# A two-block transformer kernel: matrix products on the stream before its norm, in the first stage of the latent attention and in the token pooling

## The reference

```python
def rmsnorm(x, g):
    y = x * lax.rsqrt(jnp.mean(x * x, axis=-1, keepdims=True) + 1e-6)
    return y * g

# end of the first block, start of the second
x = x + 0.5 * swiglu(rms_norm(x, ffn2_norm), ...)
x = rms_norm(x, final_norm)
h = concatenate([meta_tokens, x])                 # 16 + 512 tokens
a = rmsnorm(h, norm_mix_pre[0]);  lat = a @ w_dqkv # latents of the attention, 672 columns
...
# second layer of the second block
a = rmsnorm(h, norm_mix_pre[1])
# pool_mixer: 4 groups of 256 features, windows 2, 4, 8, 16
pooled[t, g] = sum(a[t-w+1 .. t, g]) / min(t + 1, w)
mixed = pooled - a
y = einsum('blgc,gcd->blgd', mixed, w_group) * scale
h = h + rmsnorm(y, norm_mix_post[1])
```

## Time and profile before

| | us |
|---|---|
| median of 3 runs (lowest, highest) | 2468.05 (2458.19, 2468.3) |
| the profiled execution's own time | 2468.25 |
| its span, first to last instruction | 2466.5 |
| PE busy, share of the span | 2308.9, 94% |
| DVE, ACT, POOL busy | 1069.0, 910.1, 998.1 |

### The profile page before, as it was taken

The page is one execution under the profiler, slowest core; times in us unless marked ns, Lnnn a source line. Parts: engine busy times, 40 slices in busy tenths (PEclk is TensorE's granted clock), DMA queues, the critical chain, the costliest instruction groups (busy, mean ns, idle before and its releaser), DMA issues.

```text
span 2466.5 us, 35997 instructions
## 1 busy us (share of the span) xinstructions
PE 2308.9 (94%) x14099; PEld 2027.3 (82%) x14099; DVE 1069.0 (43%) x1584; ACT 910.1 (37%) x1656; POOL 998.1 (40%) x758
## 2 busy tenths in 40 slices
PE   8999999999889899999988999799999938999999
PEld 6888887777677678888877888799999837999999
DVE  3313134564432242231356563562644475626354
ACT  4323235313353342222354453542433335424243
POOL 3445454532363344444531112244444432444443
PEclk9999999998899999999999999899999968999999
DMA  4333323321242123333211011133232201333221
GB/s 145 94 97 95 94 81 91 86 69 35 86 137 69 52 84 96 94 94 94 86 56 32 28 35 49 48 93 94 86 94 84 79 9 57 89 94 94 86 88 67
DMA packets 355686, 193.61 MB, mean 78 GB/s; under 512 B 7357, under 2 KB 350034, under 8 KB 355554
## 3 DMA queue, kind: packets, MB, share of 16 engines
q1 hardware_dynamic: 355026, 190.61, 26.4%
q10 hardware_dynamic: 528, 1.19, 0.2%
HBM read 189.67 MB, written 2.10 MB: 78 GB/s over the span
## 4 chain that ended last, share of the span: by engine, by line
PE 82%; DVE 11%; ACT 4%; issue 2%; DMA 0%; DVEq 0%; ACTq 0%; SPq 0%; POOL 0%
PE PS L544 22%; PE PS L546 22%; PE PS L548 22%; PE PS L1966 2%; PE PS L566 2%; PE PS L1984 1%; DVE u_conv L908 1%; PE PS L2038 1%; PE PS L2020 1%; ACT w_hi L490 1%; DVE g_conv L908 1%; PE PS L1155 1%; DVE hid L919 1%; PE PS L1567 1%; DVE u_conv L911 1%
## 5 line engine op out<-in xcount | busy, mean ns | idle before, releaser
L477 POOL TENSOR_TENSOR w_lo<-raw,w_hi 128x512 fp32r<-128x512 f32 (+4 forms) x743 | 976.4, 1336 | 1417.9 <-ACT w_hi L490 1417.9
L544 PE MATMUL PS<-XHI,w_hi 128*128 128x512 f32 (+2 forms) x2632 | 741.8, 332 | 41.0 <-DVE XLO L644 37.0
L490 ACT ACTIVATE w_hi<-raw 128x512 fp32r<-128x512 f32 (+4 forms) x743 | 412.5, 604 | 943.4 <-PE PS L548 879.4
L546 PE MATMUL PS<-XLO,w_hi 128*128 128x512 f32 (+2 forms) x2632 | 731.6, 328 | 0.0
L548 PE MATMUL PS<-XHI,w_lo 128*128 128x512 f32 (+2 forms) x2632 | 729.0, 327 | 0.0
L544 PEld LDWEIGHTS PS<-XHI,w_hi 128*128 128x128 f32 x2632 | 446.8, 190 | 97.4 <-issue 45.2
L546 PEld LDWEIGHTS PS<-XLO,w_hi 128*128 128x128 f32 x2632 | 444.7, 190 | 46.3 <-issue 2.9
L548 PEld LDWEIGHTS PS<-XHI,w_lo 128*128 128x128 f32 x2632 | 445.0, 190 | 43.6
L544 PE MATMUL PS<-h_hi,w_hi 128*128 128x512 f32 (+2 forms) x1056 | 282.3, 321 | 5.9 <-DVE h_lo L921 5.8
L546 PE MATMUL PS<-h_lo,w_hi 128*128 128x512 f32 (+2 forms) x1056 | 281.6, 321 | 0.0
L548 PE MATMUL PS<-h_hi,w_lo 128*128 128x512 f32 (+2 forms) x1056 | 281.5, 321 | 0.0
(11 more groups left out here) (294 smaller groups left out, 2404.3 us busy)
## 6 DMA issues: line engine op xcount, KB each, us to landing
raw<-in_ffn_w_up SPq DMA_DIRECT2D x132, 512.0 KB, 3.7
raw<-in_ffn_w_down SPq DMA_DIRECT2D x64, 512.0 KB, 3.8
raw<-in_ffn_w_gate SPq DMA_DIRECT2D x44, 512.0 KB, 3.8
raw<-in_w_in SPq DMA_DIRECT2D x25, 512.0 KB, 3.7
raw<-in_ffn_w_down SPq DMA_DIRECT2D x32, 384.0 KB, 3.4
raw<-in_xattn_w_kv SPq DMA_DIRECT2D x16, 512.0 KB, 3.7
raw<-in_w_out SPq DMA_DIRECT2D x8, 512.0 KB, 3.7
raw<-in_xattn_w_q SPq DMA_DIRECT2D x8, 512.0 KB, 4.4
```

Source lines behind the costliest of these rows:

```text
L477: ins = nc.gpsimd.tensor_tensor(d, r, h.bitcast(F32), ALU.subtract)
L490: ins = nc.scalar.activation(d, r, ACT.Copy)
L544: nc.tensor.matmul(ps, wh, ahi(k)[:, c:c + w], start=(k == 0), stop=False)
L546: nc.tensor.matmul(ps, wh, alo(k)[:, c:c + w], start=False, stop=False)
```

## The change

Two stages are rearranged; the arithmetic that is asked for stays the same.

In the first, PE's attention units are computed on the stream before `final_norm`, with the gains of `final_norm` and of the pre-norm multiplied into one (`fin_g`). Both norms' factors become one factor behind the product: the mean of squares of x times the `final_norm` gain, plus eps times the first norm's mean square. The meta tokens, which have no final norm, get their squares (`meta_sq`) and gained values (`meta_t`) early, in the first FFN. The splits of the stream's tiles move into the last units of the FFN, the second norm's squares are added up by DVE and summed by one `pe_norm` behind the second unit, and the final norm's own factor and the scaling of `X` by it are moved into the attention's steps (`dve_fin_x`).

In the second, PE multiplies the group weights with the stream before its norm and before the pooling, which commute with the product. The splits of `X` start in the post-norm. The factor and the window sums follow on the evacuated product (`grouped`), all on DVE; POOL's window sums and the tile `mixed` are gone.

```diff
-    PE_SUMMED = (S_FFN1, S_MLA, S_CF0, S_POOL, S_POOLP, S_CF1)
+    PE_SUMMED = (S_FFN1, S_CF0, S_POOL, S_POOLP, S_CF1)
...
+        (dve_rows, behind the copies of the gains)
+        link(nc.vector.tensor_tensor(meta_t[:, :, :], x_meta, x_meta, ALU.mult))
+        link(nc.vector.tensor_reduce(meta_sq[:, :], meta_t[:, :, :].rearrange("p k t -> p t k"), AX.X, ALU.add))
+        nc.vector.tensor_tensor(meta_t[:, :, :], x_meta, pre.to_broadcast([P, KD, META]), ALU.mult).then_inc(cols_ready, 1)
+        nc.vector.tensor_tensor(fin_g[:, :], column("final_norm", None, 0, KD), pre, ALU.mult).then_inc(cols_ready, 1)
...
+    def act_fin_split(act, m, j):
+        ...
+        nc.scalar.activation(XHI[:, m, META:S2], xt(m, 1), ACT.Identity, scale=fin_gain(m)).then_inc(x_hi, 1)
+        act_square(act, S_FIN, m, j, xt(m, 1), S1)
+    def dve_fin_split(dve, m, j):
+        ...
+        nc.vector.scalar_tensor_tensor(XLO[:, m, META:S2], xt(m, 1), fin_gain(m), XHI[:, m, META:S2].bitcast(F32), ALU.mult,
+                                       ALU.subtract).then_inc(x_lo, 1)
+        dve_acc(dve, S_FIN, m, j, S1)
     def act_fin(act):
-        act_sqrt(act, S_FIN, S1)
         for k in range(KD):
-            x_ready.wait(act, ("fin", k))
-            act_split(act, D_MLA, k, k, 2, G_PRE[0])
-            act_square(act, S_MLA, k, k, X[:, k, :], S2)
+            if k == KD // 2:
+                hi_to(act, PHASE["mla"] + 2)
+            act.wait_ge(acc_done, KD * S_MLA + k - 1)
+            nc.scalar.activation(sq[:, k % 2, 0:S1], xt(k, 1), ACT.Square, scale=G_FIN(k)).then_inc(sq_done, 1)
+        hi_to(act, PHASE["mla"] + 3)
+        act.wait_ge(norm_ms, S_MLA + 1)
+        act_rsqrt(act, sd[:, 0:S2], ms[:, 0:S2]).then_inc(norm_sd, 2)
     def dve_fin(dve, link):
-        dve_norm(dve, link, S_FIN, (PHASE["ffn2"] + 68) % 4, 1)
-        (per tile: scale X by gain and factor, L1716; dve_split)
+        (fin_ms from PSUM; ms of the stream = fin_ms * EPS, of the meta tokens EPS)
+        (per tile: acc += sq; then ms += mean of the second sum, and the Newton step)
+    FIN_X_AT = {14: 0, 24: 1, 34: 2, 44: 3, 54: 4, 64: 5, 70: 6, 74: 7}
+    def dve_fin_x(dve, link, x):
+        if x == 5:
+            dve.wait_ge(fin_sd, 1)
+            newton(link, fin_rn[:, :], fin_ms, rt[:, 0:S1], fin_rn[:, :])
+        if x in FIN_X_AT:
+            k = FIN_X_AT[x]
+            link(nc.vector.scalar_tensor_tensor(xt(k, 1), xt(k, 1), G_FIN(k), fin_rn[:, :], ALU.mult, ALU.mult))
...
     def pe_mla(pe):
-        pe_first_unit(pe, n, S_MLA, D_MLA, 2, n)
-        for j in range(1, 6):
+        for j in range(6):
+            if j == 0: pe.wait_ge(meta_lo, 1)
+            if j == 2: pe.wait_ge(norm_ms, S_FIN + 1)
             if j == 3:
                 pe.wait_ge(norm_ms, S_MLA + 1)
             pe_unit(pe, n + j, ...)
+            if j == 0: pe_norm(pe, S_FIN, (n + 2) % 4, 1).then_inc(norm_sum, 1)
+            if j == 1: pe_norm(pe, S_MLA, (n + 3) % 4, 2).then_inc(norm_sum, 1)
...
     def act_mla(act):
-        hi_to(act, n + 2)
-        act_sqrt(act, S_MLA, S2)
...
         act_m.inc(ins, "krope")
+        act_rsqrt(act, fin_rn[:, :], fin_ms).then_inc(fin_sd, 1)
         hi_to(act, n + 3)
...
     def pe_pool(pe):
-            if g == 1:
-                pe.wait_ge(norm_ms, S_POOL + 1)
-            (two pe_square of the group before)
+        pe.wait_ge(norm_ms, S_POOL + 1)
+        for m in range(KD):
             pe_square(pe, S_POOLP, SUMS, 2, m)
     def act_pool(act):
-        (per group: split mixed; evacuate to M and square the group before; hi_to(n + g + 1))
+        act_sqrt(act, S_POOL, S2)
+        for g in range(4):
+            hi_to(act, n + g + 2)
+            evacuate(g)                      # to grouped
+        for m in range(KD):
+            pool_mixed.wait(act, m)
+            act_square(act, S_POOLP, m, m, M[:, m, :], S2)
     def dve_pool(dve, link):
+        for k in range(3):
+            dve_split(dve, D_POOL, k, 2, G_PRE[1])
+        dve.wait_ge(acc_done, KD * (S_POOL + 1))
+        (ms)
+        for k in range(3, KD):
+            dve_split(dve, D_POOL, k, 2, G_PRE[1])
+        (Newton step)
+        for g, win in enumerate(WINDOWS):
+            for k in tiles:
+                pool_out(dve, k)
+                link(nc.vector.tensor_tensor(pa[:, k, 16:], grouped[:, k, :], rn[:, 0:S2], ALU.mult))
+            src = window_sums(... on DVE, for all four groups ...)
+            (correct the first 16 tokens, two instructions)
+            for i, k in enumerate(tiles):
+                pool_mixed.inc(nc.vector.scalar_tensor_tensor(M[:, k, :], src[:, i, 16:], 1.0 / win, pa[:, k, 16:], ALU.mult,
+                                                              ALU.subtract), k)
...
-        act_post(act, 1, S_CF0P, S_POOL)
-        act_sqrt(act, S_POOL, S2)
+        act_post(act, 1, S_CF0P, S_POOL, D_POOL, G_PRE[1])
```

More of the change, by code:

```diff
@@ L605, in program @@
     dve_end.declare(("x_out", 1), "ms", ("x_out", 2), ("x_out", 3))
-    x_ready.declare("meta", *[("x", k) for k in range(KD)], *[("fin", k) for k in range(KD)])
+    x_ready.declare("meta", *[("x", k) for k in range(KD)])
     def act_loop(act, count, body):
@@ L758, in pe_rows, with dve_rows @@
         turned.inc(ins, "cols")
-    def dve_rows(dve):
+    def dve_rows(dve, link):
         turned.wait(dve, "cols")
@@ new lines, in act_fin @@
+            act.wait_ge(acc_done, KD * S_MLA + k - 1)
[3 more added lines that the diff above has]
+        act_rsqrt(act, sd[:, 0:S2], ms[:, 0:S2]).then_inc(norm_sd, 2)
+    def dve_fin(dve, link):
+        dve.wait_ge(norm_sum, len([x for x in range(S_FIN + 1) if x not in PE_SUMMED]))
+        fin_sum = PS[(PHASE["mla"] + 2) % 4][:, 0, :]
+        nc.vector.tensor_scalar(fin_ms, fin_sum, 1.0 / D, EPS, ALU.mult, ALU.add).then_inc(norm_ms, 1)
+        link(nc.vector.memset(ms[:, 0:META], EPS))
+        nc.vector.tensor_copy(acc[:, 0:META], meta_sq[:, :])
+        dve.wait_ge(norm_ms, S_FIN + 1)
+        link(nc.vector.tensor_scalar(ms[:, META:S2], fin_ms, EPS, None, ALU.mult))
+        for k in range(KD):
+            dve.wait_ge(sq_done, KD * S_MLA + k + 1)
+            to = acc[:, META:S2]
+            if k == 0:
+                nc.vector.tensor_copy(to, sq[:, 0, 0:S1]).then_inc(acc_done, 1)
+            else:
+                dve.wait_ge(acc_done, KD * S_MLA + k)
+                nc.vector.tensor_tensor(to, to, sq[:, k % 2, 0:S1], ALU.add).then_inc(acc_done, 1)
+        dve.wait_ge(norm_sum, len([x for x in range(S_MLA + 1) if x not in PE_SUMMED]))
+        nc.vector.scalar_tensor_tensor(two(ms[:, 0:S2]), psv((PHASE["mla"] + 3) % 4, 2), 1.0 / D, two(ms[:, 0:S2]), ALU.mult,
+                                       ALU.add).then_inc(norm_ms, 1)
+        dve.wait_ge(norm_sd, S_MLA + 1)
+        newton(link, rn[:, 0:S2], ms[:, 0:S2], rt[:, 0:S2], sd[:, 0:S2])
@@ L2116, in dve_mla @@
         n = PHASE["mla"]
-        dve_norm(dve, link, S_MLA, (n + 3) % 4, 2)
         R = rn[:, 0:S2]
@@ L2190, in dve_mla @@
                 scaled(*at)
+            dve_fin_x(dve, link, x)
             if evac_at(x):
@@ L2247, in pe_pool @@
             s = (n + g) % SPLIT
-            for k in range(2):
-                pe.wait_ge(x_lo, KD * D_POOL + 2 * g + k + 1)
+            pe.wait_ge(x_lo, KD * D_POOL + 2 * g + 2)
             for mt in range(2):
@@ L2375, in _ @@
+        pool_mixed.wait(dve, KD - 1)
     @block.sync
```

134 lines of the change are left out of this document (47 added, 87 removed).

## The result

The changed kernel takes 2437.07 us (median of 4 runs, 2435.75 to 2440.21); the kernel before, run beside it, takes 2466.18 us (4 runs, 2458.19 to 2468.3). The ratio is 0.9896 with a 95% interval of 0.988 to 0.9912: about 1% faster, a small gain but clear of the noise. In later comparisons, each on another chip of the same kind, the kernel before had medians of 2462.5 to 2463.9 us over 7 to 11 runs, so the three runs the prediction started from lay some 4 to 6 us high.

What follows compares the result with a forecast made beforehand. PE was taken to bound the long FFNs, DVE's chain the pooling. 12.5 - 0.3 + 10.6 = 22.8 us off the profiled 2468.25 gave 2445.4; set against the median 2468.05, the forecast was 2445, range 2435 to 2456.

Steps and rivals of the forecast that it cites:

- The sum: Whole kernel: 12.5 us from the first stretch, minus 0.3 in the attention, plus 10.6 in pooling, 22.8 us off.
- First stretch: End of first block to sixth attention unit: splits under the FFN let PE run on, 12.5 us saved.
- term for the clock: First stretch: PE's stall behind unit 1 lowers its clock, 0.9 us taken off the gain.
- the rival of one stretch only: Latents queue behind the factor or attention covers fail, leaving 5 us or less of 12.5: 2453 us; chance 0.18.
- Attention: Final norm's factor and eight scalings moved there are hidden in idle time, costing 0.3 us; uncovered 8.2.
- Pooling: Pooling stage: group products leave the chain, which is DVE's, Newton ending at 2038.8 instead of 2049.4; 10.6 us saved.
- contention: Pooling: POOL's 7.9 us of weight rests slow DVE by 0.65 us per us of overlap, 5.1 us.
- the full lock: Pooling rival: POOL's whole 7.9 us blocks DVE, losing 2.8 to 5 us more, 2448 to 2450; chance 0.10.
- The tail: Pooling's end: ACT squares 0.64 us, PE's sum at lower clock 3.6, then 5.6 to the end of Newton.
- The rival of the warm tail: POOL hardly touches DVE, two sums at full clock: pooling gains 5 + 1.8 us more, 2437 us; chance 0.15.
- The slower rival: Pooling's chain, all on DVE, runs at contended pace, 61 us instead of 26.4: 2475 us; chance 0.04.

Runs made afterwards that it cites:

- after_again: The changed kernel once more, no edit, timed in a later job; 2439.91 us, ratio 0.9907 to the kernel before.
- a_only: The changed kernel with the pooling stage of the kernel before, so only the first stage's part of the change; 2449.91 us, ratio 0.9943.
- no_fin_x: The changed kernel without the final norm's own factor, its Newton step and the eight scalings of the stream in the attention; 2439.5 us, ratio 0.9902.
- b_only: The kernel before with the pooling stage of the changed kernel; 2451.4 us, ratio 0.9953.
- late2: The changed kernel with two last-FFN weight units' pieces issued behind pooling's last square, ahead of the last norm's root; 2437.38 us, ratio 0.9898.
- warm_pool: The changed kernel with unused filler matmuls on PE between and behind the last squares of the pooling; 2434.97 us, ratio 0.9884.
- all_three: The changed kernel with the edits of late_weights and warm_pool, and the second norm's squares gathered in `rn` instead of `acc`; 2437.32 us, ratio 0.9895.
- combo_warm: The changed kernel with late2's edit, second norm's squares gathered in `rn`, POOL's clearing two units later, and fillers as in warm_pool; 2431.93 us, ratio 0.9871.
- late_weights: The changed kernel with two last-FFN weight units' pieces issued behind pooling's squares, one ahead of the last root, one behind; 2439.02 us, ratio 0.9896.

## Why the prediction was right, point by point

**The sum** was 22.8 us (12.5 - 0.3 + 10.6); the rows give 23.4 (13.5 - 1.1 + 11.3 - 0.3), and two later comparisons 24.0 (after_again) and 26.4 (parts added). The mechanism and its size were right. The time came out 8 us lower than predicted for two reasons outside the sum: the base of 2468 was 2 to 6 us above the medians that more runs of the kernel before give (2462.5 to 2466.2), and the changed kernel's own two medians differ by 2.8 us. That the sum comes within 0.6 us of the rows is in part luck: terms that were off by 0.6 to 1 us lie on both sides of it, as the next points show.

**First stretch, 12.5 predicted, 13.5 measured.** In time after the FFN's end: the final norm's sum starts at 5.7 us (predicted 5.9) and takes 1.02 us (1.1); unit 1 ends at 12.5 (12.9); PE waits 3.5 us (4.2), predicted as a wait of some 4 us for `acc`; unit 4 starts at 30.7 (30.4), and the sixth unit is read at 42.7 (42.7 without the clock, 43.6 with it). The wait was 0.7 us shorter and the sum behind it, at the lower clock, 1.0 us longer than I had them (2.13 instead of 1.1), and the factor was ready 23.9 us after the FFN's end, as in the sum. Without its term for the clock the sum gave 42.7 for the sixth unit, which is what was measured: the 0.9 us taken off for the clock is the term that was mis-sized, since the slow sum and pairs lay beside the wait of unit 4 for its weights, and the 0.5 us that unit 5 was to wait for its own did not come. Against the rival of one stretch only, no unit is late, which a_only confirms at 42.7.

**Attention, 0.3 predicted.** The factor took 3.9 us on ACT as said, and the weight split stood behind it. ACT's timeline, after:

```profile
1289.20 1.28 ACT L675 ACT_TABLE_LOAD   x1
...
1292.44 0.63 ACT L676 ACTIVATE fin_rn<-fin_rn 128x512 f32<-128x512 f32 x1
1292.98 1.01 ACT L495 ACTIVATE w_hi<-raw 128x576 fp32r<-128x576 f32 x3
```

no_fin_x shows that nothing of it is on the path. Over the attention's steps nothing is lost at all: DVE's last `mst<-mst` row (the scale of the 80th step) starts 201.5 us after the sixth unit's read before, and 201.35 in the changed kernel and in no_fin_x. So the 0.3 us predicted there are not to be seen, and the 1.1 us by which the whole stretch is longer lie behind the attention, where the kernels are alike. Between that row and the first addition of squares to `acc` behind it before takes 19.4 us and the changed kernel 20.9. PE waits 1.21 us for `XLO` in both just ahead of the attention's output products, and then runs them at full clock in the one and at the lower clock in the other. By stage, before (columns as above):

```profile
1510.60:1514.60 4.00, 3.81 (x31) 3.81 (x32) 1.42 (x3) 1.69 (x3) 2.01 (x2) 1.00 0.01 4
```

after:

```profile
1488.00:1492.00 4.00, 3.96 (x20) 3.96 (x21) 1.22 (x2) 1.68 (x3) 1.52 (x2) 0.57 0.03 6
```

and after_again, which has the same instructions as after:

```profile
1492.00:1496.00 4.00, 3.87 (x31) 3.87 (x32) 1.36 (x3) 1.69 (x3) 2.06 (x2) 1.00 0.02 6
```

So it is a fall of the clock that need not come with the change. The eleven other kernels with the first part, after among them, have it (0.57 to 0.60 there), b_only and before do not. after_again, without it, loses its 0.8 us further on, and late2 and warm_pool, the longest at 672.7 and 672.9, have a second stretch at the lower clock, 275 to 280 us after the sixth unit's read (0.81, where before and after have 1.00). Why the clock falls in one kernel's profile and not in another's behind the same wait is open.

**Pooling, 10.6 predicted, 11.3 measured (10.1 to 11.1 by the parts).** The order is as described: products directly behind the squares' sum, PE idle beside squares (15 us in four waits; I had said about 20), sums of 1.3 us. DVE's chain from the first `pa` to the last `M` was 26.4 us uncontended in my sum. late2 measures 26.7 with one pair of POOL's pieces left beside it, which makes the first two `pa` 2.33 us instead of 1.44: 25.8 without. In the changed kernel it is 30.7 (predicted 31.5 with contention), so contention costs 4.9 us in the chain, and 0.8 more in two steps of Newton ahead of it (1.13 and 1.12 us where 0.71 is free): 5.7 against 5.1 in the sum. Counted as in the sum, by what the pieces take free (7.9 us for the four), the price is 0.72 a us where I had 0.65. late2 took two units' pieces, 5.0 us free, and 4.0 us of the chain away, 0.8 a us.

Why this is less than the full lock, which the rival put at 7.9 us, the rows show too. The second `pa` pair and the pieces at 1983.58 together take 3.73 us (1983.58 to 1987.31); alone they take 1.44 and 2.49, 3.93 in all. The two times add up as if the engines worked by turns, but the loss is shared: the pieces are longer as well (3.16 against 2.49; those of 256 columns 2.74 and 1.90 against the 1.43 of the earlier trace rows), 2.5 us over the four rows. The Trainium skill ("SBUF — State Buffer", section "Who interferes with whom") calls it an exclusive lock, and the trace agrees; what was wrong is to book the whole of POOL's time to DVE, as the rival did. The tail was cold, as taken, but shorter: the last `M` ends at 2007.23, the squares' sum at 2010.87, 3.6 us, and from there to the end of Newton at 2016.5 it is 5.7 us, 9.3 in all against 9.9 in the sum, mostly because PE began 0.1 us behind the last `M` where I had put 0.64 us of ACT in between. This is the 0.7 us between 10.6 and 11.3: the last `M` itself came where the sum had it, 37.8 us after the squares' sum (37.9). The rival of the warm tail, which would have been needed for 2437 by its mechanism, did not happen; the time near it is reached by the two reasons given with the sum.

**The slower rival** needed a chain above 54 us; it was 30.7.

**The 9.1 us ahead of the change.** Busy time by stage in the mixer, before (columns as above):

```profile
570.00:575.00 5.00, 5.00 (x20) 4.49 (x20) 1.49 (x5) 0.26 (x1) 0.00 (x0) 0.50 0.00 0
```

and after:

```profile
570.00:575.00 5.00, 5.00 (x30) 4.19 (x29) 2.13 (x2) 1.15 (x2) 1.47 (x2) 1.00 0.01 3
```

PE is fully busy in both (and so from 565 to 570), at 0.50 (1.2 GHz) before and 1.00 (2.4 GHz) after. Its work there is small products, many of 64x64. Such an additional stretch at the lower clock stands in the profiles of before, after_again, all_three and combo_warm, at 560 to 590 us, and in none of the other ten; the second FFN ends at 1237.2 to 1242.4 in those four and at 1233.1 to 1238.2 in the others. after_again, all_three and combo_warm hold the change, so the stretch does not belong to the kernel before; whether the change makes it rarer is not shown, with one profile of the kernel before.

Rows of ACT show how the 9.1 us come about. The first `g_act` of the first FFN starts at 40.25 before and at 37.74 after: 2.5 us, there as soon as the FFN's first results are read. In the other kernels with the first part this row lies at 37.6 to 39.7, in b_only at 39.66, so it varies by 2 us with the same instructions. It grows to 3.1 us within that FFN (`g_act` at 313.63 and 310.54) and to 4.6 us at the `dec` row of the mixer (445.86 and 441.25). From there to the load of `mem_in` behind the slow stretch (624.63 and 615.82) it grows to 8.8. So 4.2 of the 9.1 us come in the part that holds the slow stretch, 2.5 at the start, and the rest in small steps. None of it was predicted.

## What to carry to other kernels

Where an engine idles for a norm's factor and the products are linear in the stream, run the products on the un-normed stream and multiply at the evacuated result: the stretch before and the factor's chain then overlap. Price the freed stretch by what becomes late next (here a second sum, 3.3 us with the clock behind it), and put the other engine's work neither beside the chain nor beside the next one, but in the gap between them: moving the pieces to the wrong gap gave back 1.9 of 4.0 us (late_weights), to the right one nothing (late2). Judge a change of 3 us by the stretches between fixed events, and not by medians that wander by 3: the first stretch repeats to 0.1 us. Where PE idles and the clock falls and rises, as in the pooling stage, the same instructions still differed by 1.5 us between profiles (74.9 and 76.4), so look at the rows that make up the difference too.
